# Two-layer hybrid decoder trunk on one core: squares of the first norm summed by TensorE, rotary tables moved into VectorE's loop, four buffers for the shift weights

## The chip, the cores and the metric

The kernel runs on one core of one Trainium2 chip. The metric is the device time of one execution in microseconds (us), the median of several runs. Matmuls are on TensorE (PE; its weight loads stand apart as PEld), elementwise work on VectorE (DVE), ScalarE (ACT) and GpSimd (POOL); SP issues most transfers.

## The reference

Two layers, model width 1024, sequence 1024, batch 1, all in float32:

```python
c_act = jax.nn.silu(c)
for l in range(DEPTH):
    mod = (c_act @ w_ada[l] + b_ada[l])[:, None, :]
    sh1, sc1, g1, sh2, sc2, g2 = jnp.split(mod, N_MOD, axis=-1)
    h = rms_norm(x, norm1_g[l]) * (1.0 + sc1) + sh1
    z = h @ w_in[l]
    u, cq_in, ckv_in, kr_in, gate_a, gate_b = jnp.split(z, split_pts, axis=-1)
    y_a = s5_mixer(u, ...) @ w_a_out[l]
    y_b = mla_mixer(cq_in, ckv_in, kr_in, positions, cos, sin, ...) @ w_b_out[l]
    merged = jax.nn.sigmoid(gate_a) * y_a + jax.nn.sigmoid(gate_b) * y_b
    x = x + g1 * (merged @ w_out[l])
    h = rms_norm(x, norm2_g[l]) * (1.0 + sc2) + sh2
    x = x + g2 * ((jax.nn.silu(h @ w_gate[l]) * (h @ w_up[l])) @ w_down[l])
return rms_norm(x, final_g)
```

`cos` and `sin` of the positions are the rotary tables; the attention masks by position. Only the work ahead of the first `h @ w_in` is touched by the change: the mean of the squares of x, `sh1` and `sc1` of layer 0, the mask and the rotary tables.

## The kernel before

x lies transposed in `x_sb`: eight tiles k of 128 channels by 1024 positions; the positions are worked in two halves of 512. Each engine has its own instruction list, written out by hand, and counting semaphores between them; an engine does its list strictly in order, so that a wait holds up everything behind it. A float32 product is made of three matmuls of rounded parts (`whi`, `wlo`, `h_hi`, `h_lo`): ScalarE makes `whi` from the loaded weights `raw` (`split_hi`, L520), GpSimd the rest `wlo` (`split_lo`, L528).

What runs before the first such product:

- **SP** loads constants, the eight tiles of x (L624), and then for each k one tile of `w_first` into `first_raw` (L630, two buffers) and one tile of the first `w_ada` into `shift_raw` (L633, two buffers). Each load waits until its buffer is free: `first_mm` counts TensorE's steps, `shift_used` DVE's. Behind these come the state-space parameters (L621) and the first units of `w_in` (L539).
- **TensorE** multiplies for each k eight blocks of `first_raw` with one column of the activated conditioning (L1040): this is `sc1`, in PSUM bank 0. Then `mean_squares(0, 0)` (L1049) takes the mean over channels of the squares of half 0, `norm_scale(0, 0)` (L1058) spreads the reciprocal root over the partitions, and the first gate products (`early_gate`, L544 to L547) follow. `mean_squares(0, 1)` for half 1 stands between them.
- **ScalarE** squares x tile by tile into the four slots of `sq_ring` (L1526, two slots a half), takes the sine of both angle arrays (L1550, L1551), makes one mask row block a step (L1553), then both first weight splits, the root `std` (L1532) and the copy `rb` (L1513), then `h_hi` (L1541).
- **GpSimd** adds the squares of k = 1 to 7 of each half into `sq_sum` (L864), and then splits the weights.
- **DVE** makes the angles, then for k = 0 to 7 one mask step `mask_t` (L1964) and one product with a sum over the row for `sh1` (`row_products`, L1906), then six steps for the rotary tables `tq` and `tk` (L1969 to L1974), the modulation columns (L1978 to L1984), the reciprocal (L1990), and the hidden tiles: `t_ring` (L1998) and `h_lo` (L2006).

```python
            for k in range(1, KT):
                for t in range(2):
                    add_squares(0, 0, t, k)
```

## Time and profile before

| what | value |
|---|---|
| median of three runs | 3301.49 us |
| the three runs | 3297.54, 3302.95, 3301.49 us |
| the profiled execution, its own time | 3297.22 us |
| its span on the core | 3295.4 us |
| TensorE busy | 3127.7 us (95%) |
| DVE, ScalarE, GpSimd busy | 1607.0, 1031.3, 1005.1 us |

The span is the stretch between the first and the last instruction of the profiled execution; its own time has 1.8 us around it. Starts are counted from the start of the span. Matmuls of float32 with one column are shown as two rows each, so the 64 matmuls of L1040 are 128 rows.

### The profile page before, as it was taken

Reading aid. Unit: us, or ns where it says so; the run is one execution under the profiler, and the core shown is the slowest. Engines: PE = TensorE matmul, PEld = TensorE weight load, DVE = VectorE, ACT = ScalarE, POOL = GpSimd, SP = SyncE. Lnnn points to the kernel's source line nnn. Section 1 sums busy time; section 2 is a strip of 40 time slices with the busy share of each in tenths; the row PEclk is TensorE's granted clock in tenths of the full one; section 3 lists DMA queues with packets and bytes.
Section 4 is the critical chain, followed back from the end, with each engine's and each line's share of the span. In section 5 each row is a group of like instructions: output and inputs, shape, how many; then the busy total and the mean of one; then the engine's idle time right before and its main releaser. Section 6 shows DMA issues by size and latency. Waiting matters only on the chain.

```text
span 3295.4 us, 38057 instructions
## 1 busy us (share of the span) xinstructions
PE 3127.7 (95%) x15392; PEld 2651.2 (80%) x15392; DVE 1607.0 (49%) x1987; ACT 1031.3 (31%) x1474; POOL 1005.1 (31%) x582
## 2 busy tenths in 40 slices
PE   5899989999999999999988999899899999999998
PEld 4788878988778888888877888799777888888886
DVE  8697547865142333233277872778532232223224
ACT  3333347762131111111142333677312211111112
POOL 4456322232322222222246551223214222222223
PEclk9899989999999999999999999999999999999999
DMA  7454400014322122211134542001241111111111
GB/s 257 138 163 148 136 30 17 20 49 134 115 71 64 58 68 67 64 58 52 45 135 147 158 158 82 10 15 48 75 166 45 45 45 52 45 52 45 52 45 71
DMA packets 250213, 267.15 MB, mean 81 GB/s; under 512 B 34753, under 2 KB 204865, under 8 KB 248514
## 3 DMA queue, kind: packets, MB, share of 16 engines
q1 hardware_dynamic: 243424, 222.90, 22.0%
q10 hardware_dynamic: 6626, 41.95, 3.3%
q8 instruction: 118, 1.93, 0.3%
q14 instruction: 45, 0.37, 0.0%
HBM read 220.69 MB, written 44.11 MB: 80 GB/s over the span
## 4 chain that ended last, share of the span: by engine, by line
PE 85%; DVE 6%; issue 4%; ACT 3%; POOL 1%; DMA 1%; SPq 0%; DVEq 0%; POOLq 0%; ACTq 0%
PE ps L544 22%; PE ps L546 21%; PE ps L547 21%; PE ps L1313 3%; PE ps L1297 2%; PE ps L1302 2%; PE ps L1301 2%; PE ps L1334 2%; PE ps L1333 2%; PE ps L1103 1%; PE ps L1105 1%; PE ps L1104 1%; PE ps L1136 1%; PE ps L1148 1%; DVE x_sb L2385 1%
## 5 line engine op out<-in xcount | busy, mean ns | idle before, releaser
L528 POOL TENSOR_TENSOR wlo<-raw,whi 128x1024 fp32r<-128x1024 f32 (+4 forms) x294 | 561.8, 1919 | 1905.9 <-ACT whi L520 1905.1
L520 ACT ACTIVATE whi<-raw 128x1024 fp32r<-128x1024 f32 (+4 forms) x294 | 247.1, 862 | 1694.0 <-PE ps L547 1631.9
L544 PE MATMUL ps<-h_hi,whi 128*128 128x512 f32 x2048 | 658.2, 398 | 30.5 <-DVE h_lo L2006 17.4
L546 PE MATMUL ps<-h_lo,whi 128*128 128x512 f32 x2048 | 649.7, 393 | 0.0
L547 PE MATMUL ps<-h_hi,wlo 128*128 128x512 f32 x2048 | 648.3, 393 | 0.0
L544 PEld LDWEIGHTS ps<-h_hi,whi 128*128 128x128 f32 x2048 | 383.8, 190 | 115.2 <-DVE h_lo L2006 16.8
L547 PEld LDWEIGHTS ps<-h_hi,wlo 128*128 128x128 f32 x2048 | 389.3, 190 | 83.1
L546 PEld LDWEIGHTS ps<-h_lo,whi 128*128 128x128 f32 x2048 | 388.8, 190 | 81.2
L2367 DVE TENSOR_TENSOR silu<-silu,ps 128x1024 f32<-128x1024 f32 x44 | 53.7, 1221 | 769.5 <-PE ps L547 760.2
L2385 DVE SCALAR_TENSOR_TENSOR x_sb<-ps,mod,x_sb 128x1024 f32<-128x1024 f32 x160 | 203.3, 1280 | 178.2 <-PE ps L547 178.2
L544 PE MATMUL ps<-hid_hi,whi 128*128 128x512 f32 x704 | 224.9, 393 | 9.6 <-DVE x_sb L2385 9.6
L546 PE MATMUL ps<-hid_lo,whi 128*128 128x512 f32 x704 | 222.4, 390 | 0.0
L547 PE MATMUL ps<-hid_hi,wlo 128*128 128x512 f32 x704 | 222.1, 389 | 0.0
L1894 DVE TENSOR_TENSOR pt_lo<-ps,pt_hi 128x512 fp32r<-128x512 f32 x256 | 164.6, 685 | 35.1 <-ACT pt_hi L1513 34.4
L2296 DVE CUSTOM_DVE_ANT_0 ps<-ps,mask 128x1024 f32<-128x1024 f32 x128 | 157.3, 1229 | 20.7 <-PE ps L1302 18.5
L544 PEld LDWEIGHTS ps<-hid_hi,whi 128*128 128x128 f32 x704 | 130.6, 188 | 43.9 <-DVE x_sb L2385 18.0
L1513 ACT ACTIVATE pt_hi<-ps 128x512 fp32r<-128x512 f32 x256 | 139.1, 596 | 81.0 <-PE ps L1313 79.3
L547 PEld LDWEIGHTS ps<-hid_hi,wlo 128*128 128x128 f32 x704 | 132.2, 188 | 27.9
L546 PEld LDWEIGHTS ps<-hid_lo,whi 128*128 128x128 f32 x704 | 132.2, 188 | 27.9
L1760 ACT ACTIVATE probs<-ps,neg_max 128x1024 f32<-128x1024 f32 x128 | 143.6, 1122 | 16.5 <-DVE neg_max L2296 16.4
L1313 PE MATMUL ps<-ident,probs 128*128 128x128 f32 x1024 | 133.3, 273 | 0.6 <-ACT probs L1760 0.5
L1333 PE MATMUL ps<-pt_hi,v_st 128*128 128x256 f32 x512 | 128.0, 283 | 2.8 <-DVE pt_lo L1894 1.6
(273 smaller groups left out, 4924.1 us busy)
## 6 DMA issues: line engine op xcount, KB each, us to landing
ada_raw<-in_w_ada SPq DMA_DIRECT2D x64, 512.0 KB, 4.3
raw<-in_w_in SPq DMA_DIRECT2D x100, 256.0 KB, 3.6
raw<-in_w_gate SPq DMA_DIRECT2D x88, 256.0 KB, 3.3
raw<-in_w_up SPq DMA_DIRECT2D x88, 256.0 KB, 3.3
raw<-in_w_down SPq DMA_DIRECT2D x88, 256.0 KB, 2.9
gate_scratch<-gst ACTq DMA_DIRECT2D x32, 512.0 KB, 3.4
gl<-gate_scratch SPq DMA_DIRECT2D x32, 512.0 KB, 4.0
xs_scratch<-x_sb ACTq DMA_DIRECT2D x2, 4096.0 KB, 12.4
```

Of the source, the lines that this page charges most:

```text
L520: last = act.activation(dst(whi[:, s, :]), src(raw[:, s, :]), ACT.Copy)
L528: last = pool.tensor_tensor(dst(wlo[:, s, :]), src(raw[:, s, :]), dst(whi[:, s, :].bitcast(F32)), ALU.subtract)
L544: pe.matmul(o, w_h, x_h, start=first, stop=False)
L546: pe.matmul(o, w_h, x_l, start=False, stop=False)
L547: return [pe.matmul(o, w_l, x_h, start=False, stop=last) for o, (x_h, _) in zip(outs, xs)]
L1313: last = pe.transpose(ps[:, 4 + t, k * P:(k + 1) * P], probs[:, T % 2, kt * P:(kt + 1) * P], ident[:, 0:P])
L1333: pe.matmul(out_, v_both, pt_hi[:, n % 2, k, :], start=(k == 0), stop=False)
L1513: return act.activation(dst, src, ACT.Copy)
L1760: act.activation(probs[:, r % 2, :], pair(2 * (r % 2)), ACT.Exp, bias=neg_max[:, r % 2:r % 2 + 1], scale=-1.0, accum_out=row_sum[:, r // T ...
L1894: return dve.tensor_tensor(out, value, hi.bitcast(F32), ALU.subtract)
L2296: dve.tensor_tensor_reduce(out=s, in0=s, in1=mask[:, step % TT, :], scale=1.0, scalar=3e38, op0=ALU.add, op1=ALU.min, accum_out=neg_max[:, ...
L2385: dve.scalar_tensor_tensor(x_sb[:, t, :], pair(2 * (t % 2)), mod[:, 5, t:t + 1], x_sb[:, t, :], ALU.mult, ALU.add).then_inc(dn_ev.sem, 1)
```

## The change

- SP: `shift_raw` has four buffers, each with a semaphore of its own, and its load of step k waits for the product of step k - 4 instead of k - 2. The state-space parameters are loaded behind the first two units of `w_in`. The mask's temporary buffer moves to another place in memory.
- TensorE: in each step k, ahead of the eight matmuls on `first_raw`, eight matmuls take the squares straight from `sq_ring` and add their mean into PSUM bank 6. `mean_squares(0, 0)` and `mean_squares(0, 1)` go.
- GpSimd: the fourteen additions into `sq_sum` of the first norm go. Everything later stays.
- ScalarE: the squares run one step ahead of the mask, the root is taken ahead of the last mask step, and both weight splits go behind the copy `rb`, among the first hidden tiles.
- DVE: the rotary tables are made between the fourth and the fifth `shift` product, and the reciprocal ahead of the last one. The signal that the tables are ready is given behind the first hidden tiles.

```diff
--- before.py
+++ after.py
@@ -304,7 +304,7 @@
 
         place(32)
         first_raw = sb("first_raw", [P, 2, D])
-        shift_raw = sb("shift_raw", [P, 2, D])
+        shift_raw = sb("shift_raw", [P, 4, D])
         hi_bias = sb("hi_bias", [P, TT])
         lo_bias = sb("lo_bias", [P, TT])
         pos_i = sb("pos_i", [P, SEQ], I32)
@@ -317,9 +317,10 @@
         sin_t = sb("sin_t", [P, SEQ])
         pos_i2 = sb("pos_i2", [P, SEQ], I32)
         pos_lo = sb("pos_lo", [P, SEQ])
-        mask_t = sb("mask_t", [P, 2, SEQ])
         first_c = sb("first_c", [P, D])
         assert where[0] <= zero + 96 * K
+        place(12)
+        mask_t = sb("mask_t", [P, 2, SEQ])
         place(32)
         fin = sb("fin", [P, KT, SEQ])
 
@@ -354,7 +355,7 @@
         angles_ready = count("angles_ready", 0)
         first_loaded = [count("first0_loaded", 0), count("first1_loaded", 0)]
         first_mm = count("first_mm", 0)
-        shift_loaded = [count("shift0_loaded", 0), count("shift1_loaded", 0)]
+        shift_loaded = [count(f"shift{n}_loaded", 0) for n in range(4)]
         shift_used = count("shift_used", 0)
         c_stored = count("c_stored", 0)
         c_loaded = count("c_loaded", 32)
@@ -628,10 +629,9 @@
 
                     sp.wait_ge(first_mm.sem, k - 1)
                 sp.dma_start(first_raw[:, s, :], w_first[k * P:(k + 1) * P, :]).then_inc(first_loaded[s].sem, 16)
-                if k >= 2:
-                    sp.wait_ge(shift_used.sem, k - 1)
-                sp.dma_start(shift_raw[:, s, :], w_ada[0][k * P:(k + 1) * P, :]).then_inc(shift_loaded[s].sem, 16)
-            s5_parameters(0)
+                if k >= 4:
+                    sp.wait_ge(shift_used.sem, k - 3)
+                sp.dma_start(shift_raw[:, k % 4, :], w_ada[0][k * P:(k + 1) * P, :]).then_inc(shift_loaded[k % 4].sem, 16)
 
             for l in range(DEPTH):
                 w_in_l = w_in[l]
@@ -653,6 +653,8 @@
 
                 for t in range(2):
                     gate_unit(U_PRE + t, t)
+                if l == 0:
+                    s5_parameters(0)
                 for n in range(4):
                     load_unit(sp, l, U_U + n, u_unit(n))
 
@@ -864,9 +866,6 @@
                 pool.tensor_tensor(total, sq_ring[:, 2 * t, :] if k == 1 else total, sq_ring[:, 2 * t + k % 2, :],
                                    ALU.add).then_inc(sq_added[t].sem, 1)
 
-            for k in range(1, KT):
-                for t in range(2):
-                    add_squares(0, 0, t, k)
             for t in range(2):
                 split_lo(pool, 0, U_PRE + t)
             for l in range(DEPTH):
@@ -1035,6 +1034,20 @@
             pe.wait_ge(pool_const.sem, 2)
             pe.wait_ge(act_const.sem, 1)
             for k in range(KT):
+                for half in range(2):
+
+                    pe.wait_ge(sq_ready[half].sem, k + 1)
+                    for t in range(4 * half, 4 * half + 4):
+                        last = pe.matmul(ps[:, 6, t:t + 1], sq_ring[:, 2 * half + k % 2, (t - 4 * half) * P:(t - 4 * half + 1) * P],
+                                         mean_col[:, :], start=(k == 0 and t == 0), stop=(k == KT - 1),
+                                         skip_group_check=True)
+                        if t % 4 == 2 and k:
+                            last_read = last
+                    if k == KT - 1:
+                        last_read.then_inc(sq_added[half].sem, 1)
+                        last.then_inc(sq_mm.sem, 1)
+                    elif k:
+                        last.then_inc(sq_added[half].sem, 1)
                 pe.wait_ge(first_loaded[k % 2].sem, 16 * (k // 2 + 1))
                 for n in range(KT):
                     last = pe.matmul(ps[:, 0, n:n + 1], first_raw[:, k % 2, n * P:(n + 1) * P], c_act[:, k:k + 1],
@@ -1060,7 +1073,6 @@
                                      start=True, stop=True)
                 last.then_inc(rb_mm.sem, 1)
 
-            mean_squares(0, 0)
             norm_scale(0, 0)
             for l in range(DEPTH):
 
@@ -1079,7 +1091,8 @@
                 early_gate(1, 0)
                 early_gate(1, 1)
                 early_gate(0, 3)
-                mean_squares(l, 1)
+                if l:
+                    mean_squares(l, 1)
                 early_gate(1, 2)
                 early_gate(0, 4)
                 early_gate(0, 5)
@@ -1542,22 +1555,27 @@
                                bias=mod[:, 3 * (o // 2), k:k + 1]).then_inc(h_hi_done.sem, 1)
 
             act.wait_ge(x_in_loaded.sem, 16 * KT)
+            for t in range(2):
+                square(0, 0, t, 0)
+            act.wait_ge(angles_ready.sem, 1)
+            act.activation(sin_t[:, :], ang[:, :], ACT.Sin).then_inc(act_const.sem, 1)
+            act.activation(ang_k[:, :], half[:, :], ACT.Sin).then_inc(act_const.sem, 1)
             for k in range(KT):
-                for t in range(2):
-                    square(0, 0, t, k)
-                if k == 0:
-                    act.wait_ge(angles_ready.sem, 1)
-                    act.activation(sin_t[:, :], ang[:, :], ACT.Sin).then_inc(act_const.sem, 1)
-                    act.activation(ang_k[:, :], half[:, :], ACT.Sin).then_inc(act_const.sem, 1)
+                if k + 1 < KT:
+                    for t in range(2):
+                        square(0, 0, t, k + 1)
+                else:
+                    wait(act, sq_mm, 0, 2)
+                    norm_std(0, 0)
                 act.wait_ge(mask_sum.sem, k + 1)
                 act.activation(mask[:, k, :], mask_t[:, k % 2, :], ACT.Relu, bias=lo_bias[:, k:k + 1], scale=MASK_UNIT)\
                     .then_inc(mask_step.sem, 1)
+            norm_rows(0, 0)
             split_hi(act, 0, U_PRE)
+            hidden_hi(0, 0, 0)
+            hidden_hi(0, 0, 1)
             split_hi(act, 0, U_PRE + 1)
-            norm_std(0, 0)
-            norm_rows(0, 0)
-            for k in range(3):
-                hidden_hi(0, 0, k)
+            hidden_hi(0, 0, 2)
             for l in range(DEPTH):
 
                 act.dma_start(xs_dram, x_sb[:, :, :]).then_inc(x_spilled.sem, 16)
@@ -1958,13 +1976,20 @@
             link(dve.tensor_scalar(lo_bias[:, :], posq_i2[:, :], -MASK_UNIT, None, ALU.mult))
 
 
-            for k in range(KT):
+            def mask_rows(k):
                 if k >= 2:
                     dve.wait_ge(mask_step.sem, k - 1)
                 dve.scalar_tensor_tensor(mask_t[:, k % 2, :], pos_f[:, :], hi_bias[:, k:k + 1], pos_lo[:, :],
                                          ALU.subtract, ALU.add).then_inc(mask_sum.sem, 1)
-                dve.wait_ge(shift_loaded[k % 2].sem, 16 * (k // 2 + 1))
-                row_products(mod[:, 0, k:k + 1], shift_raw[:, k % 2, :], first_c[:, :]).then_inc(shift_used.sem, 1)
+
+            def shift_rows(k):
+                dve.wait_ge(shift_loaded[k % 4].sem, 16 * (k // 4 + 1))
+                row_products(mod[:, 0, k:k + 1], shift_raw[:, k % 4, :], first_c[:, :]).then_inc(shift_used.sem, 1)
+
+            for k in range(4):
+                mask_rows(k)
+                shift_rows(k)
+            mask_rows(4)
             dve.wait_ge(act_const.sem, 4)
             link(dve.tensor_tensor(ang_k[:, :], ang_k[:, :], ang_k[:, :], ALU.mult))
             link(dve.tensor_scalar(ang_k[:, :], ang_k[:, :], -2.0, 1.0, ALU.mult, ALU.add))
@@ -1972,8 +1997,13 @@
             link(dve.scalar_tensor_tensor(tq[:, :], sin_t[:, :], rope_sb[:, 2:3], tq[:, :], ALU.mult, ALU.add))
             link(dve.tensor_scalar(tk[:, :], ang_k[:, :], rope_sb[:, 4:5], None, ALU.mult))
             link(dve.scalar_tensor_tensor(tk[:, :], sin_t[:, :], rope_sb[:, 5:6], tk[:, :], ALU.mult, ALU.add))
-            dve.wait_ge(mask_step.sem, KT)
-            dve.sem_inc(tables_ready.sem, 1)
+            for k in range(4, KT):
+                shift_rows(k)
+                if k + 1 < KT:
+                    mask_rows(k + 1)
+                if k == KT - 2:
+                    dve.wait_ge(std_ready.sem, 1)
+                    dve.reciprocal(rstd[:, 0, 0:4], std[:, 0, 0:4]).then_inc(rstd_ready.sem, 1)
             dve.wait_ge(shift_used.sem, KT)
             dve.tensor_tensor(mod[:, 0, :], mod[:, 0, :], cols[:, 0, ROW_B_ADA:ROW_B_ADA + KT], ALU.add)\
                 .then_inc(mod_ready.sem, 1)
@@ -2008,10 +2038,11 @@
 
             wait(dve, a1_ready, 0, 0)
             dve.wait_ge(c_stored.sem, 16)
-            norm_inverse(0, 0)
             hidden_scaled(0, 0, 0)
             for k in range(2):
                 hidden_lo(0, 0, k)
+            dve.wait_ge(mask_step.sem, KT)
+            dve.sem_inc(tables_ready.sem, 1)
             for l in range(DEPTH):
                 dve.tensor_copy(pcol[:, :], cols[:, l, :]).then_inc(pcol_ready.sem, 1)
                 wait(dve, pcol_ready, l, 1)
```

The order of TensorE's instructions from its first matmul on, before:

```order
L1040 MATMUL ps<-c_act,first_raw 128x1 [waits first0_loaded,act_const,pool_const]
L1040 MATMUL ps<-c_act,first_raw 128x1 x7
L1040 MATMUL ps<-c_act,first_raw 128x1 [waits first1_loaded]
L1040 MATMUL ps<-c_act,first_raw 128x1 x7
L1040 MATMUL ps<-c_act,first_raw 128x1 [waits first0_loaded]
```

and in the changed kernel:

```order
L1041 MATMUL ps<-columns,sq_ring 128x1 [waits sq0_ready,act_const,pool_const]
L1041 MATMUL ps<-columns,sq_ring 128x1 x3
L1041 MATMUL ps<-columns,sq_ring 128x1 [waits sq1_ready]
L1041 MATMUL ps<-columns,sq_ring 128x1 x3
L1053 MATMUL ps<-c_act,first_raw 128x1 [waits first0_loaded]
L1053 MATMUL ps<-c_act,first_raw 128x1 x7
L1041 MATMUL ps<-columns,sq_ring 128x1 [waits sq0_ready]
L1041 MATMUL ps<-columns,sq_ring 128x1 x3
L1041 MATMUL ps<-columns,sq_ring 128x1 [waits sq1_ready]
L1041 MATMUL ps<-columns,sq_ring 128x1 x3
L1053 MATMUL ps<-c_act,first_raw 128x1 [waits first1_loaded]
L1053 MATMUL ps<-c_act,first_raw 128x1 x7
```

Eight one-column matmuls on the squares now stand ahead of each eight on `first_raw`, with a wait for ScalarE's squares ahead of each four.

ScalarE from the last pair of squares on (`whi` is a weight split, `rb` the spread reciprocal), before:

```order
L1553 ACTIVATE mask<-mask_t,lo_bias 128x1024 [waits mask_sum]
L1526 ACTIVATE sq_ring<-x_sb 128x512 [waits sq0_added]
L1526 ACTIVATE sq_ring<-x_sb 128x512 [waits sq1_added]
L1553 ACTIVATE mask<-mask_t,lo_bias 128x1024 [waits mask_sum]
L520 ACTIVATE whi<-raw 128x1024 [waits raw0_loaded]
L520 ACTIVATE whi<-raw 128x1024 [waits unit_used,raw1_loaded]
L1532 ACT_TABLE_LOAD
L1532 ACTIVATE std<-ps,columns 128x4 [waits sq_mm]
L1513 ACTIVATE rb<-ps 128x512 [waits rb_mm]
```

and in the changed kernel:

```order
L1539 ACTIVATE sq_ring<-x_sb 128x512 [waits sq0_added]
L1539 ACTIVATE sq_ring<-x_sb 128x512 [waits sq1_added]
L1571 ACTIVATE mask<-mask_t,lo_bias 128x1024 [waits mask_sum]
L1545 ACT_TABLE_LOAD [waits sq_mm]
L1545 ACTIVATE std<-ps,columns 128x4 [waits sq_mm]
L1571 ACTIVATE mask<-mask_t,lo_bias 128x1024 [waits mask_sum]
L1526 ACTIVATE rb<-ps 128x512 [waits rb_mm]
L521 ACTIVATE whi<-raw 128x1024 [waits raw0_loaded]
L1554 ACTIVATE h_hi<-t_ring,mod 128x512 [waits t_ready] x2
L521 ACTIVATE whi<-raw 128x1024 [waits unit_used,raw1_loaded]
L1554 ACTIVATE h_hi<-t_ring,mod 128x512 [waits t_ready]
```

Both weight splits have moved from ahead of the root to behind `rb`, one on each side of two `h_hi`; the root stands ahead of the last mask step.

DVE from the end of its second to last step of the loop on (`ISA` on `shift_raw` is the product for `sh1`), before, where the list has come to the last `mod` and the tables:

```order
L1964 SCALAR_TENSOR_TENSOR mask_t<-pos_f,hi_bias,pos_lo 128x1024 [waits mask_step]
L1906 ISA shift_raw,mod<-shift_raw,first_c 128x1024 [waits shift1_loaded]
L1906 ISA mod 128x1
L1969 TENSOR_TENSOR ang_k<-ang_k 128x1024 [waits act_const]
L1970 TENSOR_SCALAR ang_k<-ang_k 128x1024 [waits dve_const]
L1971 TENSOR_SCALAR tq<-ang_k,rope_sb 128x1024 [waits dve_const]
L1972 SCALAR_TENSOR_TENSOR tq<-sin_t,rope_sb,tq 128x1024 [waits dve_const]
L1973 TENSOR_SCALAR tk<-ang_k,rope_sb 128x1024 [waits dve_const]
L1974 SCALAR_TENSOR_TENSOR tk<-sin_t,rope_sb,tk 128x1024 [waits dve_const]
L1978 TENSOR_TENSOR mod<-mod,cols 128x8 [waits dve_const,mask_step,shift_used]
L1981 TENSOR_TENSOR mod<-ps,cols 128x8 [waits first_mm]
L1984 SCALAR_TENSOR_TENSOR a_56<-mod,cols 128x8 [waits mod_ready]
```

and in the changed kernel, in the second half of the loop:

```order
L1982 SCALAR_TENSOR_TENSOR mask_t<-pos_f,hi_bias,pos_lo 128x1024 [waits mask_step]
L1924 ISA shift_raw,mod<-shift_raw,first_c 128x1024 [waits shift2_loaded]
L1924 ISA mod 128x1
L1982 SCALAR_TENSOR_TENSOR mask_t<-pos_f,hi_bias,pos_lo 128x1024 [waits mask_step]
L2006 RECIPROCAL rstd<-std 128x4 [waits std_ready]
L1924 ISA shift_raw,mod<-shift_raw,first_c 128x1024 [waits shift3_loaded]
L1924 ISA mod 128x1
L2008 TENSOR_TENSOR mod<-mod,cols 128x8 [waits shift_used]
L2011 TENSOR_TENSOR mod<-ps,cols 128x8 [waits first_mm]
L2014 SCALAR_TENSOR_TENSOR a_56<-mod,cols 128x8 [waits mod_ready]
L2028 SCALAR_TENSOR_TENSOR t_ring<-x_sb,a_56,rb 128x512 [waits rb_ready,c_stored,a1_ready]
```

The tables are no longer between the last product and the modulation columns; the reciprocal stands ahead of the last product.

## Rows read from the trace of the kernel before

**Rows 1.** The page, part 1: busy time of each engine.

```profile
span 3295.4 us, 38057 instructions
PE 3127.7 (95%) x15392; PEld 2651.2 (80%) x15392; DVE 1607.0 (49%) x1987; ACT 1031.3 (31%) x1474; POOL 1005.1 (31%) x582
```
**Rows 2.** Chain of waits, 20 to 92 us: start, duration, what.

```profile
22.39 1.28 DVE mask_t L1964
...
26.02 2.21 DVE shift_raw L1906
...
64.59 1.30 DVE tk L1974
66.76 2.09 PE ps L1058 x8
...
69.51 0.76 DVE t_ring L1998
```
**Rows 3.** Lines, 18 to 67 us: busy us, mean ns | idle before, releaser.

```profile
L864 POOL TENSOR_TENSOR sq_sum<-sq_sum,sq_ring 128x512 f32<-128x512 f32 x12 | 26.6, 2250 | 0.0
```
**Rows 4.** Timeline, TensorE: start, busy, row; products on first_raw, and first squares.

```profile
19.40 6.95 PE L1040 MATMUL ps<-c_act,first_raw 128*128 128x1 f32 x32 [19.40 <-DMA first_raw<-in_w_first]
...
53.72 1.87 PE L1049 MATMUL ps<-columns,sq_sum 128*128 128x1 f32 x8 [3.15 <-POOL sq_sum L864]
```
**Rows 5.** Windows: busy us (rows) by engine, granted clock, DMA share, GB/s.

```profile
19.40:26.40 7.00, 6.95 (x32) 6.86 (x32) 6.76 (x12) 4.20 (x6) 0.94 (x1) 1.00 0.65 241
26.70:50.60 23.90, 21.44 (x96) 20.93 (x96) 23.90 (x18) 12.68 (x18) 23.90 (x12) 1.00 0.81 264
```
**Rows 6.** TensorE's weight loads of L1040: ns min/median/max.

```profile
L1040 PEld LDWEIGHTS ps<-c_act,first_raw x128: 285/333/338, 19.4 to 50.2; 128*128 128x128 f32 x128
```
**Rows 7.** Timeline, TensorE: squares of half 1, and the next matmul.

```profile
77.62 0.95 PE L1049 MATMUL ps<-columns,sq_sum 128*128 128x1 f32 x8
78.43 0.49 PE L544 MATMUL ps<-h_hi,whi 128*128 128x512 f32 x1
```
**Rows 8.** Timeline, ScalarE and SP: the squares' start and transfers issued.

```profile
18.01 1.15 ACT L1526 ACTIVATE sq_ring<-x_sb 128x512 f32<-128x512 f32 x2 [7.77 <-DMA x_sb<-in_x]
...
30.33 0.33 SPq L630 DMA_DIRECT2D first_raw<-in_w_first  x1
...
34.58 3.49 PEld L1040 LDWEIGHTS ps<-c_act,first_raw 128*128 128x128 f32 x16 [0.53 <-DMA first_raw<-in_w_first]
```
**Rows 9.** Timeline, ScalarE: first split of weights, and later the table load.

```profile
54.27 1.06 ACT L520 ACTIVATE whi<-raw 128x1024 fp32r<-128x1024 f32 x1 [0.54 <-DMA raw<-in_w_in]
...
57.01 1.28 ACT L1532 ACT_TABLE_LOAD   x1
```
**Rows 10.** Timeline, DVE: the first product and two table steps.

```profile
23.59 1.22 DVE L1906 CUSTOM_DVE_ANT_0 shift_raw<-shift_raw,first_c 128x1024 f32<-128x1024 f32 x1
...
62.48 1.28 DVE L1972 SCALAR_TENSOR_TENSOR tq<-sin_t,rope_sb,tq 128x1024 f32<-128x1024 f32 x1
63.80 0.75 DVE L1973 TENSOR_SCALAR tk<-ang_k,rope_sb 128x1024 f32<-128x1024 f32 x1
```
**Rows 11.** GpSimd's weight split at L528, 100 to 300 us: ns min/median/max.

```profile
L528 POOL TENSOR_TENSOR wlo<-raw,whi x14: 2338/2390/2912, 106.2 to 289.5; 128x1024 fp32r<-128x1024 f32 x14
```
**Rows 12.** Timeline, 79 to 95 us: DVE and GpSimd.

```profile
79.63 1.63 DVE L2006 SCALAR_TENSOR_TENSOR h_lo<-t_ring,mod,h_hi 128x512 fp32r<-128x512 f32 x2
...
88.81 5.13 POOL L528 TENSOR_TENSOR wlo<-raw,whi 128x1024 fp32r<-128x1024 f32 x2 [26.91 <-ACT whi L520]
89.38 2.33 DVE L2006 SCALAR_TENSOR_TENSOR h_lo<-t_ring,mod,h_hi 128x512 fp32r<-128x512 f32 x1 [2.05 <-ACT h_hi L1541]
...
91.64 2.85 DVE L1998 SCALAR_TENSOR_TENSOR t_ring<-x_sb,a,rb 128x512 f32<-128x512 f32 x1
```
**Rows 13.** Timeline of TensorE: end of the first gate's rows.

```profile
81.97 0.39 PE L544 MATMUL ps<-h_hi,whi 128*128 128x512 f32 x1
...
82.65 1.05 PE L1058 MATMUL ps<-ident,rstd 128*128 128x128 f32 x8
```

## The prediction

> **What bounds the kernel now.** The page comes first. TensorE is busy for 3127.7 of the 3295.4 us [rows 1], and the rest of the program is a steady stream of products that the change leaves alone, except for three things ahead of it. So the time is decided before the stream starts, and only a shift of that start can show.
>
> The chain of waits says what sets that start. From 22.39 us to the end of `tk` at 65.9 us it is DVE alone: mask step, product, mask step, product, and then the tables [rows 2]. The first mask step takes 1.28 us and later ones and products 2.2. The lines of that stretch say why: GpSimd adds squares all the time, twelve rows of 2.25 us without idle time [rows 3]. After the tables come the modulation columns and the reciprocal, then `norm_scale` on TensorE at 66.76 us for 2.09 us, `rb` on ScalarE, and the first `t_ring` at 69.51 [rows 2].
>
> TensorE is not on this chain, but the timeline and the windows show how full it is: 32 rows of the product on `first_raw` take 6.95 us in one piece, 0.217 us each, and the other 96 rows are 21.44 busy us of 23.90 [rows 4, 5]. That work is all of one column, and it does not run fast: a weight load takes 333 ns at the median and never under 285 [rows 6]. The eight rows on squares ahead of the stream take 1.87 us, while inside the stream the same eight rows take 0.81 us from the first to the matmul behind them (77.62 to 78.43), 0.101 us each [rows 4, 7]. These are TensorE's two levels, 1.2 and 2.4 GHz. The windows' clock column shows 1.00 here [rows 5], so it can't tell them apart in this first stretch; the durations can. Unbroken work of this kind for 6.95 us, and nearly unbroken work for 24 us more, did not bring the higher level.
>
> **The change part by part.**
>
> *TensorE's loop.* It gains 64 matmuls of one column, shown as 128 rows, to the 128 that it has. Both kinds cost the same at the lower level: 0.217 us a row for the products, 1.87 / 8 = 0.23 with its tail for the squares [rows 4]. So 256 rows by 0.217 is 55.6 us. It starts with the first half tile of squares: ScalarE begins two of them at 18.01, both take 1.15 us, so the first is there at about 18.65 [rows 8]. Does anything else stop it? A tile of `first_raw` issued at 30.33 was used at 34.58, 4.25 us later [rows 8]; now a step takes 32 rows, 6.95 us, and the load for step k + 2 is issued when step k's product ends, 10.4 us ahead of its use. Hidden. ScalarE's squares run a step ahead and take 1.15 us of 6.95. Hidden; what covers them is TensorE's own length. The loop ends at 18.65 + 55.6 = 74.3 us, and `norm_scale` follows there in place of 66.76: **+7.5 us**. The eight rows of `mean_squares(0, 0)` are in the loop already.
>
> *GpSimd's additions.* They go, and DVE's steps fall back from 2.2 to 1.28 and 1.22 us [rows 2, 10]. Eight pairs are 20.0 us instead of about 32; of the six table steps three take 1.28 and three 0.75 us or less, 6.1 in all. DVE could be through at about 22.4 + 20.0 + 6.1 = 48.5 us, 49 with the gaps. That buys nothing if TensorE ends at 74.3: step 7 of the shift product waits for its load, issued behind TensorE's step 5 at about 60.4, and for the reciprocal ahead of it, which waits for both halves of step 7's squares (74.3 less 3.5 = 70.8), a table load of 1.28 us [rows 9] and the root, so about 72.6. The product then ends near 74.0, just ahead of TensorE. A reciprocal one microsecond later would move the end by as much; I count nothing.
>
> *The shift buffers and the queue of SP.* Four buffers let DVE be less in step with its loads. But SP's list is in order, and the wait for `first_mm` ahead of each pair stays; so the loads follow TensorE's 6.95 us steps whatever the number of buffers. Worth 0. The first units of `w_in` are issued behind step 7's loads, at about 61 us, and needed at 77: hidden by 12 us. The parameters behind them are not read for another 30 us.
>
> *The weight splits.* Before, ScalarE splits the first unit at 54.27 [rows 9], while everybody waits for DVE. Now both splits come after `rb`, in the middle of the hidden tiles. ScalarE's part fits: the first split of 1.06 us lies beside the 0.76 us of the first `t_ring`. GpSimd's doesn't. One split takes 2.39 us [rows 11], and DVE is stopped by it: beside two splits of 5.13 us together, two DVE operations took 2.33 and 2.85 us where one takes 0.76, so 3.7 us more [rows 2, 12]. Here two splits meet the same chain of `t_ring` and `h_lo`. It costs nothing at the least, if each falls in a wait, and 2 by 2.39 = 4.8 us at the most; I take 3.7, the row with the same two operations. Some of it is covered: DVE ended the last `h_lo` of half 0 at 79.63 + 1.63 = 81.26, and TensorE came to it only at 81.97 [rows 12, 13], so 0.7 us of slack comes off: **+3.0 us**.
>
> The Trainium skill, "SBUF — State Buffer", on the shared port pair, says that GpSimd and a DVE operation with two inputs lock each other out for a whole instruction. The rows agree (2.2 against 1.28 us), and by that rule alone the two splits would cost the full 4.8.
>
> *Mean of half 1.* Its eight rows leave the stream, 0.81 us [rows 7]. That counts only if TensorE and not DVE paces the stream there, and with the splits in it DVE does: 0 as I take it, -0.8 at the best. On the other side TensorE starts that stream with a pause at the lower clock level, up to 1.5 us more.
>
> *The signal for the tables.* It moves behind two `h_lo`, and SP waits for it only behind four units of `w_in`. No cost.
>
> **The sum**: 7.5 + 3.0 = 10.5 us. Against the profiled execution's own 3297.22 us (span 3295.4) that is 3307.7. That execution is 4.3 us under the median of the runs, 3301.49, so the median I predict is **3312.0 us**, slower. A difference of 0.2%, 6.6 us, is about what a measurement of this kernel can tell from none, so this is not far above it. Behind the start I see no slack that takes the shift: the next stop, where TensorE waits for the second set of splits, hangs on `norm_scale` of half 1, which moves with it (82.65 before, about 93.2 now [rows 13]).
>
> **The rivals.**
>
> *The clock rises in the loop: faster.* TensorE now has no gaps at all in its loop, and if that brings the higher level early, a row costs 0.101 us [rows 7]: 256 rows are 26 us and the loop ends at about 46. Then DVE decides, at about 49 to 50 us, and the first `t_ring` starts there in place of 69.51: 19.5 us gained, 3.7 given back by the splits, 0.7 more for the squares of half 1 and the slack. That is 3301.5 - 16.5 = 3285. For it: 32 rows were unbroken before, now 256 are. Against it: nothing rose in those 6.95 us, nor at 90% busy behind them [rows 5, 6]. It decides from the point where the loop's rows fall under about 0.19 us on average, which is 66.8 us at its end. The Trainium skill, "TensorE: Matmul & The Clock Gate", part 1, has the rule that this rival lives on: sustained matmul work releases the halved clock. By that rule the loop would run mostly at the full level and the kernel would be faster; the durations here speak against it for one-column matmuls.
>
> *The late splits are free: no change.* Each split falls where DVE waits for `h_hi` anyway, TensorE paces the stream, and the squares of half 1 are saved: 7.5 - 0.8 - 0.7 = 6.0 us, 3307.5. For it: the hidden tiles do have waits. Against it: the two rows of 2.33 and 2.85 us.
>
> **How the numbers follow.** The forecast gets 0.78, the free splits 0.13, the clock 0.09. The forecast's own range: at the least 7.5 + 0 - 0.8 = +6.7, at the most 7.5 + 4.8 + 1.5 = +13.8, each widened by the 2.7 us half spread of the runs: 3305.5 to 3318. I take the low end down to 3304 to hold most of the free splits, and leave the clock's case out. The chances are 0.09 faster, 0.12 within 0.2% and 0.79 slower: nearly all of the free splits is within, and a little of it over.
>
> **What would show it.** In the changed kernel's profile: weight loads of the loop at 333 ns from 18.7 us on, `norm_scale` near 74.3 and the first `t_ring` near 77.1; DVE's mask steps at 1.28 us with idle time ahead of the later products, released by loads; no GpSimd row before about 78; two DVE operations over 2 us at 78 to 84; `norm_scale` of half 1 near 93. Loop rows at 190 ns of weight load, or a loop that ends before 66.8 us, would make the prediction wrong.

## The result and the profile after

| | before | changed |
|---|---|---|
| median of eleven runs each, us | 3303.3 | 3313.54 |
| lowest and highest | 3297.54, 3303.87 | 3309.01, 3315.03 |
| profiled execution, own time and span | 3297.22, 3295.4 | 3314.18, 3312.4 |

The ratio of the medians is 1.003, with a 95% interval of 1.0021 to 1.0039: the change makes the kernel 10.2 us slower, 0.3%. The forecast was 3312.0 us, slower, with a range of 3304 to 3318.

The two spans differ by 17.0 us, more than the medians. By the start of the products for `u` (L1103 before, L1116 now) 11.2 us of that are there; the other 5.8 us lie in the 3200 us behind it. There the profiled executions of all the kernels of this study differ by up to 6.8 us: 3204.2 us from that mark to the end of the span before, 3210.0 after, and 3205.6 to 3211.0 in the experiments. The two ends of this range go with the mean granted clock of the execution: the shortest stretch has 0.981, the longest, that of the last experiment, 0.977. The profiled execution of the kernel before was a short one, 6.1 us under its median. So the spans are not compared below; the start of the `u` products is, and the medians.

The page, part 1, of the changed kernel answers to [rows 1].

```profile
span 3312.4 us, 38257 instructions
PE 3157.6 (95%) x15504; PEld 2680.1 (81%) x15504; DVE 1593.3 (48%) x1987; ACT 1031.5 (31%) x1474; POOL 975.6 (29%) x568
```

GpSimd has 14 instructions less and is 29.5 us less busy, TensorE has 112 rows more and is 29.9 us busier: the additions have changed engines. (128 rows came and the 16 rows of both `mean_squares` went.) The totals tell nothing of who waits. The chain of waits of the changed kernel does, from 17 to 105 us; columns as in [rows 2].

```profile
18.98 3.54 PE ps L1041 x16
22.52 3.41 PE ps L1053 x16
...
70.31 3.41 PE ps L1053 x16
73.72 1.93 PE ps L1071 x8
...
77.95 0.70 DVE h_lo L2036
...
80.51 2.84 DVE t_ring L2028
...
84.07 0.79 PE ps L545
...
94.02 0.91 PE ps L1071 x8
...
102.43 0.82 PE ps L1116
```

Before, DVE stood on this chain from 22.39 us to the tables [rows 2]. Now TensorE does, from the first square to `norm_scale`: sixteen pieces of sixteen rows, 3.41 us each, the first 3.54, with nothing between them. `norm_scale` starts at 73.72 in place of 66.76.

The loop's weight loads (duration in ns, least, median, most) and its window (busy us and rows of PE, PEld, DVE, ACT, POOL, then granted clock, DMA share and GB/s) answer to [rows 5, 6].

```profile
L1053 PEld LDWEIGHTS ps<-c_act,first_raw x128: 333/333/333, 22.3 to 73.3; 128*128 128x128 f32 x128
...
L1041 PEld LDWEIGHTS ps<-columns,sq_ring x128: 288/333/333, 18.9 to 69.9; 128*128 128x128 f32 x128
```

```profile
18.90:74.00 55.10, 55.02 (x258) 55.06 (x259) 29.05 (x42) 20.68 (x27) 0.00 (x0) 1.00 0.50 178
```

TensorE is busy for all of the 55.1 us, and its weight loads take the same 333 ns as before at the median, and none less than 288: all of this ran at the lower level. The clock column shows 1.00 all the same. DVE is busy for 29 of the 55 us, GpSimd not at all.

DVE's timeline in the changed kernel (start, busy, row, and in brackets the idle time ahead and who ended it) answers to [rows 10, 12].

```profile
22.47 1.28 DVE L1982 SCALAR_TENSOR_TENSOR mask_t<-pos_f,hi_bias,pos_lo 128x1024 f32<-128x1024 f32 x1
23.68 1.22 DVE L1924 CUSTOM_DVE_ANT_0 shift_raw<-shift_raw,first_c 128x1024 f32<-128x1024 f32 x1
...
37.54 1.22 DVE L1924 CUSTOM_DVE_ANT_0 shift_raw<-shift_raw,first_c 128x1024 f32<-128x1024 f32 x1 [4.74 <-DMA shift_raw<-in_w_ada]
...
70.64 0.18 DVE L2006 RECIPROCAL rstd<-std 128x4 f32<-128x4 f32 x1 [10.37 <-ACT std L1545]
...
73.75 0.17 DVE L2011 TENSOR_TENSOR mod<-ps,cols 128x8 f32<-128x8 f32 x1 [1.62 <-PE ps L1053]
...
76.41 1.41 DVE L2028 SCALAR_TENSOR_TENSOR t_ring<-x_sb,a,rb 128x512 f32<-128x512 f32 x2 [2.29 <-ACT rb L1526]
77.95 2.63 DVE L2036 SCALAR_TENSOR_TENSOR h_lo<-t_ring,mod,h_hi 128x512 fp32r<-128x512 f32 x1
80.51 2.84 DVE L2028 SCALAR_TENSOR_TENSOR t_ring<-x_sb,a,rb 128x512 f32<-128x512 f32 x1
...
90.19 1.63 DVE L2036 SCALAR_TENSOR_TENSOR h_lo<-t_ring,mod,h_hi 128x512 fp32r<-128x512 f32 x2
```

Every mask step and product is at its short time, as GpSimd is silent, and what DVE gains it spends waiting: for the load of `shift_raw`, for the root, for TensorE. Then two operations of the hidden tiles take 2.63 and 2.84 us in place of 0.76. GpSimd's timeline has one entry in that stretch, both splits. TensorE's shows the hole that they make: it waits 1.72 us for the second hidden tile, just behind its first group.

```profile
77.30 5.50 POOL L529 TENSOR_TENSOR wlo<-raw,whi 128x1024 fp32r<-128x1024 f32 x2 [75.82 <-ACT whi L521]
```

```profile
80.73 0.76 PE L545 MATMUL ps<-h_hi,whi 128*128 128x512 f32 x1 [5.10 <-DVE h_lo L2036]
...
84.07 0.79 PE L545 MATMUL ps<-h_hi,whi 128*128 128x512 f32 x1 [1.72 <-DVE h_lo L2036]
...
88.36 0.43 PE L545 MATMUL ps<-h_hi,whi 128*128 128x512 f32 x1
...
93.18 0.39 PE L545 MATMUL ps<-h_hi,whi 128*128 128x512 f32 x1
```

The first group of three matmuls of the gate starts at 80.73, the second only at 84.07, and the rows reach the spacing of the higher level at 88.56. For the lengths of that stretch before, the chain of waits of the kernel before has, behind `norm_scale` at 66.76 [rows 2], the start of the second group, the second `norm_scale` and the first product for `u`:

```profile
73.57 0.43 PE ps L544
...
82.81 0.91 PE ps L1058 x8
...
91.22 0.82 PE ps L1103
```

### The profile page after: what moved, and what is told of

Read it like the earlier page. It is cut to its first block, busy times and chain, and to the rows that moved or that the text cites. A ratio compares the mean times of both kernels' runs of the same rounds, so it can differ in the third digit from the quotient of the medians.

```text
span 3312.4 us, 38257 instructions
## 1 busy us (share of the span) xinstructions
PE 3157.6 (95%) x15504; PEld 2680.1 (81%) x15504; DVE 1593.3 (48%) x1987; ACT 1031.5 (31%) x1474; POOL 975.6 (29%) x568
## 4 chain that ended last, share of the span: by engine, by line
PE 85%; issue 5%; DVE 5%; ACT 2%; POOL 1%; DMA 1%; SPq 0%; DVEq 0%; POOLq 0%; ACTq 0%
PE ps L545 21%; PE ps L547 21%; PE ps L548 21%; PE ps L1326 3%; PE ps L1310 2%; PE ps L1315 2%; PE ps L1314 2%; PE ps L1347 2%; PE ps L1346 2%; PE ps L1116 1%; PE ps L1117 1%; PE ps L1118 1%; PE ps L1041 1%; PE ps L1053 1%; DVE x_sb L2416 1%
```

## The experiments

The marks of all kernels, from the chain of waits and the timelines, in us from the span's start: `norm_scale` of half 0, the first `t_ring`, and the first product for `u`. The times are medians with their lowest and highest, each with its ratio to the kernel before on the same chip. Where a row follows another without a gap, the chain puts its start at the modelled end of that one, 0.1 to 0.2 us behind its start in the timeline (73.72 against 73.58 for `norm_scale` of the changed kernel). The marks are the chain's, but for the `norm_scale` of the tables behind the loop, which is not on the chain and comes from the timeline.

| run | norm_scale | t_ring | u | time (lowest to highest), runs | ratio, 95% interval |
|---|---|---|---|---|---|
| before | 66.76 | 69.51 | 91.22 | 3301.88 to 3303.62 in four jobs | 1 |
| changed | 73.72 | 76.41 | 102.43 | 3313.54 (3309.01 to 3315.03), 11 | 1.003, 1.0021 to 1.0039 |
| early splits | 73.55 | 76.23 | 97.49 | 3307.41 (3303.2 to 3309.31), 11 | 1.0016, 1.0007 to 1.0025 |
| splits in first steps | 73.77 | 76.45 | 97.32 | 3307.65 (3305.13 to 3311.05), 11 | 1.0015, 1.0006 to 1.0024 |
| half 1 on GpSimd | 60.20 | 62.89 | 90.42 | 3299.06 (3296.53 to 3301.26), 11 | 0.9992, 0.9983 to 1.0001 |
| half 1 and early splits | 61.61 | 64.46 | 86.75 | 3296.56 (3293.2 to 3299.24), 11 | 0.9981, 0.9972 to 0.999 |
| two shift buffers | 73.67 | 76.35 | 101.81 | 3312.54 (3308.13 to 3313.04), 7 | 1.0028, 1.0017 to 1.0039 |
| tables behind the loop | 73.7 | 80.71 | 105.49 | 3314.47 (3313.21 to 3316.09), 5 | 1.0035, 1.0021 to 1.0048 |
| wide matmuls added | 101.24 | 103.92 | 130.07 | 3336.69 (3336.29 to 3341.72), 4 | 1.0107, 1.0091 to 1.0122 |
| warm-up ahead | 71.39 | 74.08 | 100.19 | 3309.83 (3303.55 to 3314.29), 10 | 1.0021, 1.0012 to 1.0031 |
| wide rounded squares | none | 58.59 | 79.90 | 3288.03 (3285.77 to 3290.76), 5 | 0.9953, 0.994 to 0.9967 |
| root and reciprocal in one | none | 55.15 | 73.28 | 3282.9 (3281.51 to 3286.14), 5 | 0.9938, 0.9925 to 0.9952 |

The theory was the forecast's: TensorE's loop of one-column rows is too long by seven microseconds, and the late splits stop DVE for some four more. The rivals were that the splits cost nothing, that buffers or tables matter, and that the clock can be had.

### Undo the loop for one half

TensorE sums only the squares of half 0; GpSimd adds those of half 1 as before.

```diff
-                for half in range(2):
+                for half in range(1):
...
+            for k in range(1, KT):
+                add_squares(0, 0, 1, k)
...
-                if l:
-                    mean_squares(l, 1)
+                mean_squares(l, 1)
```

> The changed kernel, but only half 0's squares are summed by TensorE in its loop; half 1's stay with GpSimd as before. Theory (TensorE's loop sets the start, 0.213 us for each of its rows): 192 rows, the loop ends at 18.98 + 41.0 = 60.0 us instead of 73.7, norm_scale there, and the time is 13 us under the changed kernel, about 3 under the one before. Rival (DVE with its order and GpSimd's additions sets the start): DVE is slowed by seven additions and norm_scale comes at 66 or later, so that the time is close to the one before.

`norm_scale` starts at 60.20, 13.5 us earlier than in the changed kernel. 64 rows of 0.213 us are 13.7: the loop's length is what sets the mark, and each row counts in full. The splits are where they were (GpSimd 5.50 us at 63.78, DVE 2.63 and 2.84 us beside them), and the time is within a measurement of the kernel before: 0.9992, 0.9983 to 1.0001.

### Undo the late splits

```diff
+                    split_hi(act, 0, U_PRE)
+                    split_hi(act, 0, U_PRE + 1)
                     wait(act, sq_mm, 0, 2)
...
             norm_rows(0, 0)
-            split_hi(act, 0, U_PRE)
-            hidden_hi(0, 0, 0)
-            hidden_hi(0, 0, 1)
-            split_hi(act, 0, U_PRE + 1)
-            hidden_hi(0, 0, 2)
+            for k in range(3):
+                hidden_hi(0, 0, k)
```

> The changed kernel with both weight splits ahead of the root again. Theory (the late splits stop DVE for 3.7 us in the middle of the hidden tiles, on top of a TensorE loop that ends at 73.7 us): the norm_scale of half 0 stays at 73.7, the first gate matmul comes 2.4 to 3 us after rb instead of 4.5, norm_scale of half 1 moves from 94.0 to about 90, and the time is 3 to 4 us under the changed kernel, some 7 us over the one before. Rival (the splits fall in waits and cost nothing): norm_scale of half 1 stays at 94 and so does the time.

The chain of waits of this kernel, at the second group of the gate and the second `norm_scale`:

```profile
80.29 0.43 PE ps L545
...
89.08 0.91 PE ps L1071 x8
```

From one `norm_scale` to the other it is 89.08 - 73.55 = 15.53 us, in the changed kernel 94.02 - 73.72 = 20.30: the late splits cost **4.8 us**. The second group takes 3.6 of them (6.74 us behind `norm_scale` here, 10.35 there). The other 1.2 is TensorE: without the pause its rows reach the spacing of the higher level at 82.68 us, in the third group, with the pause only at 88.56. (By the timeline's starts the shares are 3.8 and 1.0.) Against the kernel before of its own job the median is 5.4 us higher, in place of 10.2. The rival of free splits is out. In the new place GpSimd's splits meet the last product of DVE, but there TensorE is later still (DVE waits 1.00 us for `rb` behind it):

```profile
72.31 2.44 DVE L1923 CUSTOM_DVE_ANT_0 shift_raw<-shift_raw,first_c 128x1024 f32<-128x1024 f32 x1
```

### The splits far ahead

The first two units of `w_in` are loaded behind step 1 and split behind steps 1 and 2, while DVE waits for its own loads.

```diff
+                if k in (1, 2):
+                    split_hi(act, 0, U_PRE + k - 1)
```

> The changed kernel, only that the first two weight units are loaded behind step 1's loads and split inside the first steps of the loop. Theory (the time of the splits matters, not the place in the list): as with both splits ahead of the root, norm_scale of half 0 at 73.7 and of half 1 at 89 us, and the time 5 us under the changed kernel, near 3308; the extra loads at 25 us cost TensorE nothing in its loop of 6.8 us steps. Rival (a load of first_raw comes late behind them): the loop ends a few us later than 73.7.

GpSimd splits at 32.12 us for 5.53 us, DVE's products of steps 2 and 3 keep their 1.23 us, and the `u` products start at 97.32, the same as with the splits just ahead of the root (97.49). Nothing of the splits' cost was left there to gain.

### Both together

```diff
-                for half in range(2):
+                for half in range(1):
...
+                    split_hi(act, 0, U_PRE)
+                    split_hi(act, 0, U_PRE + 1)
```

> Both of the earlier edits together: only half 0's squares in TensorE's loop, and both weight splits ahead of the root. Theory (loop and late splits are separate costs that add): norm_scale of half 0 at 60.2 as with the first edit alone, norm_scale of half 1 near 77 (the splits alone took 4.9 us off it, 94.0 to 89.1, and 82.0 less 4.9 is 77), the time some 5 us under the run with half 1 on GpSimd alone, 3294, and 8 under the kernel before. Rival (GpSimd, which now has seven additions and the splits in the same stretch, stops DVE there as much as the late splits did): norm_scale of half 1 stays near 82 and the time near 3299.

`norm_scale` of half 1 came at 78.35 and not at 77. ScalarE's timeline shows the new wait: the splits stand ahead of the root in its list and their weights come late in this shorter loop.

```profile
56.96 1.06 ACT L521 ACTIVATE whi<-raw 128x1024 fp32r<-128x1024 f32 x1 [5.14 <-DMA raw<-in_w_in]
...
59.78 1.28 ACT L1546 ACT_TABLE_LOAD   x1
```

Still it is 3296.56 us, 5.3 below the kernel before: the idea of the change, at half its dose and with the splits kept where they were, gains 5.3 us where the whole change loses 10.2.

### Two shift buffers, and the tables' place

```diff
-        shift_raw = sb("shift_raw", [P, 4, D])
+        shift_raw = sb("shift_raw", [P, 2, D])
...
-                if k >= 4:
-                    sp.wait_ge(shift_used.sem, k - 3)
+                if k >= 2:
+                    sp.wait_ge(shift_used.sem, k - 1)
```

> The changed kernel with two shift buffers instead of four. Theory (the loads follow TensorE's steps, whatever the number of buffers): nothing moves, norm_scale of half 0 at 73.7, the same time as the changed kernel within 2 us. Rival (four buffers hide load latency for DVE): the last shift product comes later than 70.7, and norm_scale or the first t_ring with it, by one load of 4 us or so.

DVE waits 2.06 and 4.81 us ahead of the products of steps 2 and 3, with four buffers 1.93 and 4.74; the time is 3312.54. The two further buffers do nothing: the loads follow TensorE's steps.

The other experiment puts the six table steps behind the last product.

```diff
             mask_rows(4)
-            dve.wait_ge(act_const.sem, 4)
-            link(dve.tensor_tensor(ang_k[:, :], ang_k[:, :], ang_k[:, :], ALU.mult))
...
             for k in range(4, KT):
                 shift_rows(k)
...
+            dve.wait_ge(act_const.sem, 4)
+            link(dve.tensor_tensor(ang_k[:, :], ang_k[:, :], ang_k[:, :], ALU.mult))
```

> The changed kernel with the six table steps of DVE behind the last product again, as before the change. Theory (TensorE's loop has covered DVE by little: the last product ended at 71.9 us, the loop at 73.7): the tables take 6.1 us, the first t_ring moves from 76.4 to about 78.7, and all behind it by 2.3 us. Rival (TensorE sets the start and DVE has idle time to spare): nothing moves.

The first `t_ring` starts at 80.71, 4.3 us later than in the changed kernel, of which I had expected 2.3. GpSimd's first split now meets the tables' end, and a tiny DVE step, 0.17 us elsewhere, takes 2.19:

```profile
77.40 2.98 POOL L529 TENSOR_TENSOR wlo<-raw,whi 128x1024 fp32r<-128x1024 f32 x1 [75.93 <-ACT whi L521]
```

```profile
78.22 2.19 DVE L2008 TENSOR_TENSOR mod<-mod,cols 128x8 f32<-128x8 f32 x1
```

The two hidden operations behind it are free of the split (0.75 and 0.74 us), so `u` moves by only 3.1 us. The second split meets another small step, a copy of 128x87 that takes 0.19 us elsewhere:

```profile
84.25 2.37 DVE L2047 COPY pcol<-cols 128x87 f32<-128x87 f32 x1
```

Moving the tables into the loop is thus a good part of the change; it costs nothing there, since DVE has 26 us of the loop idle. Only the marks show this: the two times, with ratios of 1.0035 and 1.003, can't be told apart.

### Can the loop have the higher level?

Two experiments ask this from two sides. Both add matmuls whose result nobody reads. The first puts four float32 rows of 512 columns into every step:

```diff
+                for half in range(2):
+                    pe.matmul(ps[:, 5, :], ident[:, 0:P], x_sb[:, k, half * HALF:(half + 1) * HALF], start=True, stop=True)
```

> The changed kernel with two matmuls of 128x512 added to each of the eight steps of TensorE's loop, whose result is not used. Theory (TensorE stays at the lower of its two levels because its work there is all of one column): the wide ones bring the higher level within the loop, a one-column row falls from 0.213 to about 0.10 us, and in spite of 16 more matmuls the loop ends earlier than 73.7, at 55 to 66 us; the kernel gets faster by 8 to 18 us. Rival (the level would not rise there for any work, because the stretch is at the start of the program): 16 matmuls by some 1.7 us at the lower level (8 rows of 128 columns took 2.08 us, so 512 columns about four times 0.52 each) are 27 us more, and the kernel is slower by that much.

My theory fell here. TensorE's timeline in the profiled execution:

```profile
22.60 3.76 PE L1052 MATMUL ps<-x_sb,ident 128*128 128x512 f32 x4
26.15 3.41 PE L1055 MATMUL ps<-c_act,first_raw 128*128 128x1 f32 x16
29.43 3.55 PE L1041 MATMUL ps<-columns,sq_ring 128*128 128x1 f32 x16
```

The wide rows take 3.76 us in every step and the one-column rows stay at 3.4 a sixteen. In this execution the level did not rise; the loop is 27 us longer and so is everything behind it.

The other three executions of this kernel are not like the profiled one. They are some 5 us shorter (3336.29 to 3336.79 us against 3341.72), and their mean granted clock is 0.967 or 0.968 against 0.980. The warmed kernel below, whose record has the clock at 0.50 from 21 to 86 us, has such a mean too, 0.970. So in these three the level may have been up for some time within the loop and fallen again; no trace shows it. In time, all four are at least 34 us over the kernel before: the theory's gain is out, the claim that the wide rows leave the level alone is not shown.

The second lets TensorE come into the loop already at the higher level, by 60 matmuls of 512 columns on constants while x is being loaded:

```diff
+            pe.wait_ge(warm.sem, 2)
+            for n in range(60):
+                pe.matmul(ps[:, 5, :], warm_r[:, 0:P], warm_r[:, :], start=True, stop=True)
             pe.wait_ge(pool_const.sem, 2)
```

> The changed kernel with 60 matmuls of 128x512 with rounded operands, whose result is not used, ahead of TensorE's loop, in the time in which it waits for x. They keep TensorE busy from about 3 to 18.7 us. First theory (the rounded 128x512 products raise the level within a few us, as in the stream, and one-column work cannot hold it): the loop's first rows take about 0.10 us, later ones 0.213 again; the loop ends some us before 73.7. Second theory (once raised, unbroken work of any kind holds it): all 256 rows at about 0.10 us, the loop ends near 47, DVE's steps and the loads become the bound, and the time falls by 15 us or more. Third (the level does not rise in the first microseconds of the program for any work): the 60 matmuls take 0.43 us each, 26 us, and delay the loop by 10 us.

Windows of this kernel, columns as above, and then TensorE's timeline at the start of the loop:

```profile
19.00:21.00 2.00, 2.00 (x19) 2.00 (x20) 1.90 (x4) 2.00 (x3) 0.00 (x0) 1.00 1.02 408
21.00:22.00 1.00, 1.00 (x9) 1.00 (x8) 0.90 (x4) 1.00 (x3) 0.00 (x0) 0.70 0.93 373
22.00:26.00 4.00, 4.00 (x20) 4.00 (x21) 3.93 (x7) 1.99 (x3) 0.00 (x0) 0.50 0.35 113
26.00:60.00 34.00, 34.00 (x161) 34.00 (x161) 20.38 (x24) 12.94 (x17) 0.00 (x0) 0.50 0.43 153
```

```profile
18.91 1.92 PE L1047 MATMUL ps<-columns,sq_ring 128*128 128x1 f32 x16
20.68 2.91 PE L1059 MATMUL ps<-c_act,first_raw 128*128 128x1 f32 x16
23.46 3.55 PE L1047 MATMUL ps<-columns,sq_ring 128*128 128x1 f32 x16
```

The first sixteen rows take 1.92 us, about 0.11 each, the next 2.91, and from 23.46 on it is 3.55 and 3.41 as ever, at a granted clock of 0.50. The engine is busy without a gap in all these windows. Its last wide row ends at about 19 us, and between 21 and 22 us the granted clock falls to 0.50, the level of 1.2 GHz. This is the first of the three theories: in these traces one-column work neither brought the higher level nor held it. No execution of the changed kernel has a mean granted clock under 0.979, so none of the eleven looks like the warmed one or the three with wide rows. The head start gives 2.3 us at `norm_scale` and 2.2 at `u`; the ratios, 1.0021 and 1.003, have intervals that overlap.

### Make the rows wide, and then end them faster

The last two experiments look for a version that beats both. The squares are rounded to TensorE's rounded format and multiplied with a matrix of 1/1024, so that a wide row sums 512 positions at once and leaves the mean on all partitions; `norm_scale` of the first norm is not needed then. The splits stand in the first steps.

```diff
-                    for t in range(4 * half, 4 * half + 4):
-                        last = pe.matmul(ps[:, 6, t:t + 1], sq_ring[:, 2 * half + k % 2, (t - 4 * half) * P:(t - 4 * half + 1) * P],
-                                         mean_col[:, :], start=(k == 0 and t == 0), stop=(k == KT - 1),
-                                         skip_group_check=True)
...
+                    last = pe.matmul(ps[:, 4 + half, :], mean_r[:, :], sq_r[:, 2 * half + k % 2, :], start=(k == 0),
+                                     stop=(k == KT - 1))
...
+                    act.activation(rb[:, half_cols(o)], ps[:, 4 + o, :], ACT.Sqrt, bias=eps_col[:, :])\
+                        .then_inc(std_ready.sem, 1)
...
+                    dve.reciprocal(rb[:, half_cols(0)], rb[:, half_cols(0)]).then_inc(rb_ready.sem, 1)
```

> Another way to sum the squares: ScalarE writes them rounded, and TensorE multiplies them as a moving operand of 512 columns with a constant 128x128 matrix, so that the mean stands on all partitions at once; norm_scale of layer 0's first norm goes, the root and the reciprocal are taken over 512 columns, and the first two weight units are loaded and split inside the first steps of the loop. The squares are rounded, the rest of the computation is unchanged. Theory (TensorE's length sets the start, at the lower level): a step is 16 rows by 0.213 us and two matmuls of 0.43, 4.3 us instead of 6.8, the loop ends near 53, the first t_ring starts at 54 to 56 instead of 76.4, and the time falls to about 3286, 16 under the kernel before. Rival (the wider work raises the level): the loop ends near 45 and DVE at about 50 decides, with the first t_ring near 52. Rival on the other side (the loads of each step, 4.25 us, or the long reciprocal on DVE take over): the first t_ring not before 60.

TensorE's timeline, and DVE's row of the reciprocal:

```profile
20.33 3.41 PE L1060 MATMUL ps<-c_act,first_raw 128*128 128x1 f32 x16
23.59 1.20 PE L1052 MATMUL ps<-sq_r,mean_r 128*128 128x512 f32 x2
24.59 3.41 PE L1060 MATMUL ps<-c_act,first_raw 128*128 128x1 f32 x16
```

```profile
53.64 3.35 DVE L2023 RECIPROCAL rb<-rb 128x512 f32<-128x512 f32 x1 [0.87 <-ACT rb L1557]
```

A step is 4.27 us in place of 6.83, the loop ends near 55 us, and the time is 3288.03, near the 3286 expected. That the rows are rounded is what makes them short: two float32 matmuls of 512 columns took 3.76 us a step above, more than sixteen one-column rows, and two rounded ones take 1.20.

The first `t_ring` starts at 58.59 and not at 54 to 56. DVE is on the chain again. The splits are no longer free for it, since it waits less: beside them one product and one mask step take 3.40 and 3.37 us. And the price has moved: a reciprocal over 128x512 takes 3.35 us on DVE, twice, and both times the chain stands behind it. The last experiment takes the root and the reciprocal as one ScalarE function instead:

```diff
-                    act.activation(rb[:, half_cols(o)], ps[:, 4 + o, :], ACT.Sqrt, bias=eps_col[:, :])\
-                        .then_inc(std_ready.sem, 1)
+                    act.activation(rb[:, half_cols(o)], ps[:, 4 + o, :], ACT.Abs_reciprocal_sqrt, bias=eps_col[:, :])\
+                        .then_inc(rb_ready.sem, 1)
```

> The kernel with wide rounded squares, but ScalarE takes the reciprocal of the root in one table function, so that DVE's two reciprocals over 512 columns (3.35 us each) go. Theory (both stand on the path: one ahead of the last product, one between the halves' hidden tiles): the first t_ring starts at about 55.5 instead of 58.6, and the products of u some 6 us earlier; the time is about 3282, 6 us under the kernel with wide rounded squares and 20 under the one before. Rival (TensorE's first loop, which ends at 55.0, and the gate products are as late as DVE): 3 us or less. Only the accuracy of the first norm's scale may change.

ScalarE's row, and two pieces of the chain of waits:

```profile
52.57 0.69 ACT L1557 ACTIVATE rb<-ps,columns 128x512 f32<-128x512 f32 x1
```

```profile
51.51 3.22 PE ps L1060 x16
...
55.15 0.76 DVE t_ring L2052
```

The 0.69 us of ScalarE replace root and reciprocal, and `u` starts 6.6 us earlier, as expected. The ratios agree with it, though their intervals overlap. **3282.9 us** is 20.7 us below the kernel before, some 31 below the changed one, and the best of the study. TensorE's last product on `first_raw` and DVE end almost together now (DVE waits 0.99 us for it), and in the seventh step, at 46.87 us, TensorE had stood idle for 0.87 us for a load of `first_raw`. So more would have to come from all three.

## Why the prediction was right

**The loop.** Forecast: from 18.65 us, 256 rows of 0.217, to 74.3, +7.5. Measured: from 18.98, 54.74 us, 0.214 a row, to 73.72, **+6.96**. The step holds to half a microsecond; the undone half shows that each row is worth its full time, and the weight loads, 333 ns at the median and none under 288, that all of it ran at the lower level.

**What does not count.** GpSimd's silence gave DVE its short steps as forecast (1.28 and 1.22 us) and bought nothing. The reciprocal came at 70.64 and the last product ended at 71.9, two microseconds ahead of the forecast's 74.0; DVE then waited 1.62 us for TensorE. I had put ScalarE's table load of 1.28 us behind the last squares. It ran ahead of that wait, and the root came right behind the squares:

```profile
68.68 1.28 ACT L1545 ACT_TABLE_LOAD   x1 [10.32 <-PE ps L1041]
70.34 0.26 ACT L1545 ACTIVATE std<-ps,columns 128x4 f32<-128x4 f32 x1 [0.38 <-PE ps L1041]
```

So the forecast's near-tie was not one. Buffers: 0, by the experiment with two. Loads of `w_in` and parameters: no wait for them stands in the chain.

**The splits.** The form is as forecast: two operations over 2 us at 77.95 and 80.51, 2.63 + 2.84 - 1.52 = 3.95 us over their usual time where the row of before gave 3.7. By the rule of the Trainium skill, "SBUF — State Buffer", on the shared port pair, that the later one of the two waits for the whole instruction of the other, I had estimated up to 4.8 for two splits. The rows show 3.95 on DVE, less than that, which fits the rule as far as they tell: the first split had begun at 77.30, DVE's operation beside it at 77.95. The undone splits show 4.8 at the second `norm_scale` too, but 1.2 of this is TensorE's level, so the equal number is chance.

**Where the sum was off, and the luck in it.** From the first `norm_scale` to the second I summed +3.0 for the splits less slack; it is 20.30 us where it was 16.05, **+4.25**. Measured piece by piece: the second group of the gate starts 10.35 us behind `norm_scale`, before 6.81, so +3.54; from there to the second `norm_scale` 9.95 us, before 9.24, so +0.71. The mis-sized term is "0.7 us of slack comes off", together with the zero for "Mean of half 1". Both took DVE for the pace of that stretch. DVE had ended the last `h_lo` at 90.19 + 1.63 = 91.82 and TensorE came to that group only at 93.18, 1.4 us later: TensorE paces it. DVE's slack at the end of the stretch could not take up a stop at its start, where TensorE stood idle for DVE. So the squares of half 1 do give back their 0.79 us, and the start at the lower level costs 0.71 + 0.79 = 1.5 more than before, which I had only as an end of the range. (By the timeline's starts it is +3.75 and +0.50, and 1.3 in place of 1.5.)

The errors partly cancel: the loop is 0.5 under its term, the stretch behind it 1.25 over its own. The total is 6.96 + 3.54 + 0.71 = 11.21 us at the mark where 10.5 was forecast. That the medians differ by 10.2, even nearer to it, is luck: their interval reaches from 6.9 to 12.9 us.

**The clock's rival.** It had 0.09 and the mark of 190 ns for weight loads; the median stayed at 333 and the least was 288. The Trainium skill, "TensorE: Matmul & The Clock Gate", part 1, says that sustained matmul work releases the halved clock. For rows of one column the traces disagree: 54.7 us without a gap did not release it, and behind the warm-up such work lost it again. In the gate's stream of 512 columns, unbroken from 84.07 us, the rows were at the higher level from 88.56.

**What stays open.** Why the wide rows mixed into the loop, float32 or rounded, did not raise the level in the profiled executions, while the gate's stream did, was not settled; nor was what happened in the three shorter executions with wide float32 rows. What sets the spread of the runs was not traced either. It goes with the mean granted clock: with two shift buffers the three executions of 3308.1 to 3308.9 us have 0.981, the four of 3312.5 to 3313.0 have 0.979.

## What to carry to other kernels

Before work is moved to an engine because the engine looks idle, write down its path with the new work at the durations of that very stretch: 128 tiny rows at the lower clock level are 27 us, and they passed the chain that they were to relieve. A split or any other GpSimd operation that stops DVE belongs where DVE waits anyway; moved into a chain that starts a stream, it costs its own time and a second, slower start of the stream. When a sum must be taken on TensorE and may be rounded, give it wide rows: sixteen rounded ones of 512 columns added 0.86 us to each of eight steps (4.27 against 3.41), 7 us in all, for what 128 of one column did in 27. In float32 they would have cost more than the narrow ones (3.76 against 3.41 us a step).
